# Moving the products of C with the powers of a from VectorE to GpSimd, behind its second norm of a step

## What is computed

```
ar, ai = mag*cos(li*dt), mag*sin(li*dt)                 # a, per group and state
xr, xi = einsum('blgh,gph->blgp', u, bb)                # input times B (complex)
h[t]   = a*h[t-1] + x[t]                                # complex scan over 256 tokens
y      = einsum('blgp,ghp->blgh', hr, c_re) - einsum('blgp,ghp->blgh', hi, c_im)
y      = gelu(y + d*u); y = y * sigmoid(y @ w_glu + b_glu)
```

## Time and profile before

| | us |
|---|---|
| median of 3 runs | 956.29 (956.06 to 958.31) |
| the profiled execution, its own time | 958.21 |
| its span | 956.5 |
| PE busy | 941.8 (98% of the span) |
| DVE busy | 618.7 (65%) |
| ACT busy | 568.7 (59%) |
| POOL busy | 112.5 (12%) |
| granted TensorE clock | 1.00 throughout |

### The profile page before, as it was taken

The page is one execution under the profiler, slowest core; times in us unless marked ns, Lnnn a source line. Parts: engine busy times, 40 slices in busy tenths (PEclk is TensorE's granted clock), DMA queues, the critical chain, the costliest instruction groups (busy, mean ns, idle before and its releaser), DMA issues.

```text
span 956.5 us, 15481 instructions
## 1 busy us (share of the span) xinstructions
PE 941.8 (98%) x5811; PEld 802.1 (84%) x5811; DVE 618.7 (65%) x961; ACT 568.7 (59%) x920; POOL 112.5 (12%) x126
## 2 busy tenths in 40 slices
PE   7999999999999999999999999999999999999998
PEld 7988888888878999888888788888888888888886
DVE  5688989899898954755644655555555555465453
ACT  4689785875957745645545564555455554565332
POOL 3101002011020000000002630220021002200000
PEclk9999999999999999999999999999999999999999
DMA  8776544445344467555999996659999866655662
GB/s 287 185 185 194 156 130 136 133 128 180 112 132 134 124 194 274 181 175 188 179 165 180 175 258 166 187 155 172 168 163 168 206 164 185 177 167 159 210 215 85
DMA packets 116006, 165.81 MB, mean 173 GB/s; under 512 B 19301, under 2 KB 56298, under 8 KB 115690
## 3 DMA queue, kind: packets, MB, share of 16 engines
q1 hardware_dynamic: 99504, 159.67, 64.2%
q10 hardware_dynamic: 16442, 5.33, 2.3%
HBM read 162.86 MB, written 2.11 MB: 172 GB/s over the span
## 4 chain that ended last, share of the span: by engine, by line
PE 64%; issue 17%; DVE 6%; ACT 5%; DMA 4%; POOL 3%; ACTq 0%; SPq 0%; POOLq 0%; DVEq 0%
PE bank L455 16%; PE bank L457 16%; PE bank L456 15%; PE bank L482 3%; PE bank L483 3%; PE bank L484 3%; DVE wl L974 2%; POOL con L2115 1%; DMA raw<-in_o_w_in 1%; DMA scr<-decay_rows 1%; ACT wh L966 1%; ACT res L1075 1%; PE bank L694 1%; POOL uz L2118 1%; PE bank L665 1%
## 5 line engine op out<-in xcount | busy, mean ns | idle before, releaser
L974 DVE TENSOR_TENSOR wl<-raw,wh 128x1024 fp32r<-128x1024 f32 x295 | 363.3, 1236 | 264.4 <-ACT wh L966 263.0
L966 ACT ACTIVATE wh<-raw 128x1024 fp32r<-128x1024 f32 x295 | 310.5, 1058 | 190.9 <-PE bank L457 116.9
L455 PE MATMUL bank<-wh,xh 128*128 128x512 f32 x768 | 309.3, 403 | 1.0 <-DVE wl L974 1.0
L457 PE MATMUL bank<-wh,xl 128*128 128x512 f32 x768 | 300.4, 391 | 0.0
L456 PE MATMUL bank<-wl,xh 128*128 128x512 f32 x768 | 299.2, 390 | 0.0
L457 PEld LDWEIGHTS bank<-wh,xl 128*128 128x128 f32 x768 | 144.1, 188 | 31.6
L455 PEld LDWEIGHTS bank<-wh,xh 128*128 128x128 f32 x768 | 144.4, 188 | 28.4 <-DVE wl L974 1.5
L456 PEld LDWEIGHTS bank<-wl,xh 128*128 128x128 f32 x768 | 144.6, 188 | 27.0
L455 PE MATMUL bank<-wh,yh 128*128 128x512 f32 x256 | 100.6, 393 | 0.0
L457 PE MATMUL bank<-wh,yl 128*128 128x512 f32 x256 | 99.8, 390 | 0.0
L456 PE MATMUL bank<-wl,yh 128*128 128x512 f32 x256 | 99.6, 389 | 0.0
(11 more groups left out here) (319 smaller groups left out, 1039.9 us busy)
## 6 DMA issues: line engine op xcount, KB each, us to landing
raw<-in_o_w_in SPq DMA_DIRECT2D x128, 512.0 KB
raw<-in_e_w_in SPq DMA_DIRECT2D x130, 256.0 KB, 3.5
raw<-in_e_w_out SPq DMA_DIRECT2D x32, 512.0 KB
raw<-in_o_w_out SPq DMA_DIRECT2D x32, 512.0 KB
raw<-in_e_w_in SPq DMA_DIRECT2D x31, 512.0 KB
raw<-in_s_w_glu SPq DMA_DIRECT2D x8, 512.0 KB
res<-in_x SPq DMA_DIRECT2D x8, 256.0 KB, 6.6
res<-in_x SPq DMA_DIRECT2D x1, 2048.0 KB, 9.4
```

The source lines that it names most:

```text
L455: nc.tensor.matmul(o, l_hi, w_hi, start=first, stop=False)
L457: mm = nc.tensor.matmul(o, l_lo, w_hi, start=False, stop=last)
L966: nc.scalar.activation(wh[:, j % RING, :], raw[:, j % RING, :], ACT.Copy).then_inc(hi_done, 1)
L974: nc.vector.tensor_tensor(wl[:, j % RING, :], raw[:, j % RING, :], wh[:, j % RING, :].bitcast(F32), ALU.subtract).then_inc(lo_done, 1)
```

## The change

`s5_far` is moved from VectorE's program to GpSimd's, with the same instructions and shapes. It no longer has slots: both calls stand at the end of GpSimd's `step(i)`, behind the norm of the second half. VectorE counts its last power of a in `pw_done`, for which GpSimd waits once.

```
-TAB_SLOT, FAR_SLOT, BA_SLOT = [0, 0], [-7, -4], [-10, -4]
+TAB_SLOT, BA_SLOT = [0, 0], [-10, -4]
...
-                link(v.tensor_tensor(pi[:, 3, :], n, a, ALU.add))
+                v.tensor_tensor(pi[:, 3, :], n, a, ALU.add).then_inc(pw_done, 1)
+                dve.wait_ge(pw_done, 1)
...
-                        if FAR_SLOT[part] == at:
-                            s5_far(i, part)
...
+            def s5_far(i, r):
+
+                if r == 0 and i:
+                    pool.wait_ge(y_ps, i)
+                if r == 0 and not i:
+                    pool.wait_ge(bc_c, 4)
+                    pool.wait_ge(pw_done, 1)
+                    pool.wait_ge(zeros, 2)
+                a_ = slice(TB * i, TB * i + TB)
+
+                def times(o, f, k):
+                    x = bc_all[:, i, 2 + f, :].rearrange("p (i k h) -> p i k h", k=1, h=16).to_broadcast([P, TB, 5, 16])
+                    y = pw[:, k, :, a_].rearrange("p k (i h) -> p i k h", h=1).to_broadcast([P, TB, 5, 16])
+                    return g.tensor_tensor(o, x, y, ALU.mult)
+
+                times(cc[r], r, 0)
+                link(times(ca_t, 1 - r, 1))
+                flat_of = "p i k h -> p (i k h)"
+                g.tensor_tensor(cc[r].rearrange(flat_of), cc[r].rearrange(flat_of), ca_t.rearrange(flat_of),
+                                ALU.subtract if r else ALU.add).then_inc(cc_done, 1)
+                pool.wait_ge(cc_done, 2 * i + (r + 1))
+
             def step(i):
...
                     qk_norm(i, 1)
+                    for r in range(2):
+                        s5_far(i, r)
```

More of the change, by code:

```diff
@@ L1644, in angles @@
                     v.tensor_scalar(w, w, 0.5, -0.5, ALU.min, ALU.max).then_inc(tab_ang, 1)
[L1646 to L1665, removed]
             def s5_hold(i):
```

## The result

The changed kernel takes 970.65 us, the kernel before 956.18 in the same comparison: ratio 1.014, 95% interval 1.0128 to 1.0153. It is 14.5 us slower. The forecast was slower by 6.8 us (963.1 us, range 957.0 to 969.0), so the direction was right, and the loss is more than twice the forecast and outside its range.

A forecast was written before the change was run, and what follows sets the result against it. TensorE bounds the kernel, with VectorE nearly late at each layer-0 step's last unit. Per step -4.9 us relief, +6.5 holds, +0.2 norm waits: net 1.8, less slack, 6.8 us over four steps, 956.29 to 963.1 us; range 957.0 to 969.0.

The forecast's parts named there:

- TensorE sets the time, VectorE is nearly late at a step's last unit: Layer-0 steps: TensorE busy 941.8 of 956.5 us; VectorE's slack at the last unit 0.84, 0.3, 0.1 and 0.1 us.
- A product takes 1.24 us, a hold 1.09 us, six of them 6.5 us: Behind GpSimd's second norm: each 640-element product takes 1.24 us and holds VectorE 1.09 us, 6.5 us a step.
- the slope through the earlier trace: GpSimd's shortest two-tensor operations, 0.451 us for 128 elements and 1.041 for 512, extended at 1.54 ns an element to 640.
- the 1.4 us that the prediction set aside: Estimate for a product from the GPSIMD reference's 2.6 cycles an element; the sum would be some 4 us larger.
- 0.2 us of waiting for GpSimd's norms: Ahead of a step's last wl: VectorE comes earlier to GpSimd's norms and waits some 0.2 us for them.
- Net 1.8 us a step, less the slack: VectorE's lateness at the last unit's wl; TensorE loses 1.9, 1.5, 1.7 and 1.7 us in the four steps.
- A range of 959.5 to 968.5 us for standing of 1.0 to 1.5 us a product: The forecast's own range of time, for VectorE held 1.0 to 1.5 us by each GpSimd product; chance 0.66.
- Product times do not delay the reader: At s5_near: the products take 11.4 us and end near 230.5, the first reader starts at 235.51; no new wait.
- The signs named for GpSimd's durations: In the profile after: GpSimd's 24 products have a least time near 1.24 us and most take above 2.
- Rival 1: Layer-0 steps: VectorE's relief of 4.9 us a step without contention that matters, 954.5 to 956.3 us; 0.22 together with rival 4.
- Rival 2: Products at 1.9 us each, reader waits: about 977 us; each 0.1 us more a product is 2.4 us; 0.08 beyond 970.
- Rival 4: Half of VectorE's standing falls beside work not held up: net 0 to 0.8 us a step, 956 to 959; 0.22 with rival 1.

The follow-up runs named there:

- run without products: The kernel before with the products of C with the powers of a left out, VectorE writing a constant once instead: 956.96 us, ratio 1.0006.
- run with filler: The changed kernel with 16 transposes of the identity on TensorE ahead of its wait for ba_done at a step's last unit: 966.88 us, ratio 1.0107.
- late run: The changed kernel, but GpSimd waits with all six products of a step until VectorE has made the last unit's wl: 970.16 us, ratio 1.0143.
- half kernel: The changed kernel with the real half of the products back on VectorE, only the imaginary half on GpSimd: 958.82 us; with one or three small writes ahead, 959.09 and 959.75.

## Why the prediction was right in kind and wrong in size

- *TensorE sets the time, VectorE is nearly late at a step's last unit.* Right. The new waits are at that unit in all four steps, and nothing behind gave them back. That relief alone is worth nothing was right too (run without products).
- *A product takes 1.24 us, a hold 1.09 us, six of them 6.5 us.* Too low. Holds in the third step add up to 7.05 us: 1.02 to 1.14 us beside a multiplication, 1.38 and 1.24 us beside an addition. The multiplication's bare 1.34 us lies 0.1 us above the slope through the earlier trace rows, nearer the 1.4 us that the prediction set aside. That slope mixed two operations, since L2152 is an addition of 128 elements and L2118 a multiplication of 512. 0.5 us a step.
- *0.2 us of waiting for GpSimd's norms.* Too low. The second sum comes the whole 2.46 us of the first half sooner, but the head outputs must then wait for GpSimd's output norm (L1822 above, 0.47 us idle), and only 1.9 us are left. 0.35 us a step, in all but the first, which has no head outputs.
- *Net 1.8 us a step, less the slack.* Measured 2.54, 3.14, 2.67 and 2.68 us of TensorE between unit starts, against 1.9, 1.5, 1.7 and 1.7: 11.0 against 6.8 us. Of the second step's 3.14 us, some 0.4 us are transposes at half clock.
- *The missing term.* The sum priced a wait of TensorE at its own length and the clock at nothing, without a reason. In two of four steps the clock fell to 1.2 GHz for 3.4 us behind the wait, and the step's last unit became 1.25 and 0.81 us longer. With the transposes that is 2.4 us by the table, 3.1 us by the run with filler. Holds (2.1 us), norms (1.1 us) and clock (2.4 us) make up 5.6 us, nearly all of the 5.8 us by which the profiled execution came out above the 965.0 us forecast for it. The medians add 1.9 us, which is the scatter of the kernel before.
- *A range of 959.5 to 968.5 us for standing of 1.0 to 1.5 us a product.* The two don't go together: by the prediction's own 2.4 us for each 0.1 us a product, 1.5 us gives about 973 us. Measured holds of 1.18 us on the mean lie well inside the condition, the time lies outside the range.
- *Product times do not delay the reader.* Right: TensorE waits at `s5_near` for ScalarE alone, as before, and from the second norm's end to that of the last product it is 11.7 us, against 11.4. Run later, they do delay it. The signs named for GpSimd's durations did not come as said: the least was 1.48 us, not near 1.24, and most of the 24 lay under 2 us.
- *Rival 1 (relief wins)* was priced rightly: no gain even without contention. *Rival 2 (slower products)* was right in its rule, each 0.1 us a product 2.4 us in all, and 0.1 us is about what a hold was off. *Rival 4* did not show: all six holds fell. Its premise holds (L1831 in the late run), but no such work stood beside the products. That a product isn't always let in at once the half kernel shows, where one let five instructions pass; the holds only came later.

Left open is which engine gets in when both have work queued, and why the clock fell in the first and second step but not in the third and fourth, whose waits were as long (2.04 and 2.05 us against 1.90 and 2.15). In the late run it fell in all four, behind waits of 2.4 to 3.0 us. No version here beats the kernel before, and the run without products says that none which only relieves VectorE in these steps would.

## What to carry to other kernels

An operation moved to GpSimd is not gone from VectorE if both read SBUF, the memory on the chip that the engines share: price it as the time for which it holds VectorE's two-input instructions, here 1.02 to 1.38 us against the 0.82 us that it took on VectorE itself. Here nothing was lost only where GpSimd's work read nothing, or read so little that the holds stayed under the relief (copies, half the elements); nothing was gained anywhere. So look at the place with the least slack, not at busy shares, and ask first what a bare relief is worth. And a new wait on TensorE can cost more than its length, since the clock may fall behind it.

## What the runs showed of the hardware that I had not expected

- With both engines queued, a GpSimd product usually got in at the next boundary of VectorE's instructions (all 24 of the changed kernel), but in the half kernels the first stood 4.9 to 5.3 us, in three steps of four, while VectorE finished five instructions, until VectorE waited for a semaphore. Starting it 0.04, 0.19 or 0.50 us into a VectorE instruction made no difference.
- VectorE stood longer beside an addition of two tiles of one buffer (1.24 and 1.38 us) than beside a multiplication with broadcast operands from two buffers (up to 1.14 us). Whether the operation or the operands make the difference no run shows.
- Waits of 1.90 and 2.15 us on TensorE were followed by 3.4 us at half clock, waits of 2.04 and 2.05 us were not; 16 transposes that nobody reads, put in their place, avoided it and won about 3 us.
- Writes by GpSimd of 640 elements (0.63 us) beside VectorE's two-input instructions changed neither. Nor did GpSimd's power over 8 elements: it took 1.64 us at 224.41 us, and beside it L1791 and `wl` took 0.68 and 1.22 us.
